# The MLPs of a two-layer decoder step, in two phases: the down product of 14 of 16 blocks by Strassen, with h through DRAM

## The reference, cut to what matters

```python
D_MODEL, D_FF = 1024, 4096

def sq_relu_mlp(x, w_up, w_down):
    h = jax.nn.relu(x @ w_up)
    return (h * h) @ w_down

for l in range(2):
    x = x + mixer(l, rmsnorm(x, norm_mix[l]))
    x = x + sq_relu_mlp(rmsnorm(x, norm_ffn[l]), w_up[l], w_down[l])
```

## Time and profile before

| | us |
|---|---|
| median of 3 runs | 2365.76 |
| lowest and highest run | 2365.53, 2367.63 |
| span of the profiled execution | 2366.2 |
| TensorE busy in it | 2313.8 |
| VectorE, ScalarE, GpSimd busy | 1476.8, 976.7, 317.2 |

### The profile page before, as it was taken

One profiled execution on the slowest core, in us unless ns is written; L12 is line 12 of the kernel. 1 busy time (PEld: TensorE's weight loads), 2 busy tenths in 40 slices (PEclk: granted clock), 3 DMA queues, 4 the chain that ended last, 5 costly groups with the idle time before them and its releaser, 6 DMA issues.

```text
span 2366.2 us, 41211 instructions
## 1 busy us (share of the span) xinstructions
PE 2313.8 (98%) x16214; PEld 2215.7 (94%) x16214; DVE 1476.8 (62%) x2598; ACT 976.7 (41%) x1978; POOL 317.2 (13%) x333
## 2 busy tenths in 40 slices
PE   7999999999999999999999999999999999999998
PEld 7988998878999999999999877869999999999998
DVE  6555555579766566565666666465856656556564
ACT  4232222235543353353434454254635335334345
POOL 1000000013111111111112011013011111111113
PEclk9999999999999999999999999999999999999999
DMA  4111121101111111211212311101111111121121
GB/s 128 37 50 57 50 69 40 46 29 45 46 54 36 53 53 35 62 44 36 66 50 56 98 28 53 36 10 45 36 54 54 36 58 48 35 63 44 44 62 74
DMA packets 160983, 119.71 MB, mean 51 GB/s; under 512 B 23623, under 2 KB 140276, under 8 KB 160836
## 3 DMA queue, kind: packets, MB, share of 16 engines
q1 hardware_dynamic: 160724, 118.10, 17.1%
q10 hardware_dynamic: 144, 0.02, 0.0%
HBM read 110.94 MB, written 12.33 MB: 52 GB/s over the span
## 4 chain that ended last, share of the span: by engine, by line
PE 72%; issue 20%; DVE 5%; POOL 1%; ACT 1%; DMA 0%; SPq 0%; POOLq 0%; DVEq 0%; ACTq 0%
PE acc L2634 9%; PE acc L2632 9%; PE acc L2633 9%; PE acc L2593 8%; PE acc L2592 8%; PE acc L2594 8%; PE acc L2701 3%; PE acc L2703 2%; PE acc L2702 2%; PE acc L2722 2%; PE acc L2570 1%; PE acc L2571 1%; PE acc L2572 1%; PE acc L2745 1%; PE acc L2733 1%
## 5 line engine op out<-in xcount | busy, mean ns | idle before, releaser
L2634 PE MATMUL acc<-h_hi,w_lo 128*128 128x352 f32 x1344 | 434.7, 323 | 0.0
L2632 PE MATMUL acc<-h_hi,w_hi 128*128 128x352 f32 x1344 | 434.0, 323 | 0.0
L2633 PE MATMUL acc<-h_lo,w_hi 128*128 128x352 f32 x1344 | 431.6, 321 | 0.0
L1535 DVE TENSOR_TENSOR x_res<-x_res,acc 128x1056 f32<-128x1056 f32 x224 | 280.6, 1253 | 126.2 <-PE acc L2634 126.0
L2633 PEld LDWEIGHTS acc<-h_lo,w_hi 128*128 128x128 f32 x1344 | 254.9, 190 | 0.0
L2593 PE MATMUL acc<-x_lo,w_hi 128*128 128x264 f32 x896 | 254.6, 284 | 0.0
L2594 PE MATMUL acc<-x_hi,w_lo 128*128 128x264 f32 x896 | 254.6, 284 | 0.0
L2592 PE MATMUL acc<-x_hi,w_hi 128*128 128x264 f32 x896 | 254.5, 284 | 0.0
L2632 PEld LDWEIGHTS acc<-h_hi,w_hi 128*128 128x128 f32 x1344 | 251.8, 187 | 0.0
L2634 PEld LDWEIGHTS acc<-h_hi,w_lo 128*128 128x128 f32 x1344 | 251.8, 187 | 0.0
L2349 PE MATMUL acc<-x_hi,w_hi 128*128 128x352 f32 x576 | 193.2, 335 | 1.4 <-DVE pair L1802 1.4
(11 more groups left out here) (351 smaller groups left out, 5356.7 us busy)
## 6 DMA issues: line engine op xcount, KB each, us to landing
w_raw<-in_w_up SPq DMA_DIRECT2D x64, 512.0 KB
w_raw<-in_w_down SPq DMA_DIRECT2D x64, 512.0 KB
w_raw<-in_w_mlstm_in SPq DMA_DIRECT2D x24, 512.0 KB
x_in<-in_x_prompt SPq DMA_DIRECT2D x8, 512.0 KB, 4.6
w_raw<-in_w_mlstm_out SPq DMA_DIRECT2D x8, 512.0 KB
w_raw<-in_w_q SPq DMA_DIRECT2D x16, 256.0 KB
w_raw<-in_w_attn_out SPq DMA_DIRECT2D x16, 256.0 KB
out_y_prompt<-y_out SPq DMA_DIRECT2D x8, 512.0 KB, 2.6
```

Of the source, the lines that this page charges most:

```text
L1535: V.tensor_tensor(blocks(x_res[:, k]), blocks(x_res[:, k]), row_banks(layer, k), ALU.add).then_inc(row_taken, 1)
L2632: T.matmul(out[:, b], hi[:, c], mh[:, span(b)], start=(c == 0), stop=False)
L2633: T.matmul(out[:, b], hi[:, c], ml[:, span(b)], start=False, stop=False)
L2634: x = T.matmul(out[:, b], lo[:, c], mh[:, span(b)], start=False, stop=(c == 1))
```

## The change

The MLP has two phases now, and its loops are written out. In the first, `up(f)` runs for all 16 blocks. The finished h (after relu, square and scale) goes to a DRAM tensor `h_rows` by two DMAs per block (`store_h`); `z_even` beside `act_a`/`act_b` gives each block's quarters a place of their own in turn.

In the second, the down product of blocks 0 to 13 is one Strassen product. The output's 1024 channels, the 14 blocks and the 1056 tokens are each cut in two. There are NPROD = 7 products, each over KG = 7 groups q of 256 rows; a group is 4 pairs of banks x 2 x 2 x 3 = 48 matmuls of 264 columns (`down(q)`). The table `DOWN` says for each product which quarter of the weights, with which other added or subtracted, meets which quarter of h, with which other, and into which quarters of `x_res` the result goes. Sums of weights are made by GpSimd (`down_sum`, 1024 columns), in products 0, 2, 4, 5 and 6; sums of h by VectorE (`t_sum_of_h`, 1056 columns), in products 1, 2, 3, 4 and 6. Both operands of each group are split by ScalarE (`w_high`, `t_high_of`) and VectorE (`w_low`, `t_low_of`). `w_hi`/`w_lo` hold two groups, the h operands have a ring of three.

SP loads three quarters of h into SBUF once (b11 in product 0, b12 in 2, b22 in 3) and streams the fourth (b21) in products 1 and 6. After each product VectorE adds every finished pair of banks, straight from PSUM, to one or two places of `x_res` (`add_banks`, 528 columns; 2, 2, 1, 2, 2, 2, 1 adds per pair for the seven products); ScalarE copies none of them out. The next product's first matmul into a pair waits for these adds (`bank_added`).

Blocks 14 and 15 stay plain and come last, as before in `last_rows` and `last_down`; their h is loaded back and split during products 5 and 6, their weights are steps 49 to 52 of the same step function.

The order of VectorE, ScalarE and SP in the down phase, and TensorE's waits:

```diff
+DOWN = (((1, 0), ADD, (1, 1), (0, 0), None, None, ((1, 0, ADD), (1, 1, SUB))),
...
+ADDS = [[(mh, nh, op, m) for m in range(4) for mh, nh, op in outs] for *_, outs in DOWN]
```

VectorE:

```diff
+            def down_step(layer, q):
+                w_low(layer, q)
+                if q + 1 < NG:
+                    t_low_of(layer, q + 1)
+                if q + 2 in T_SUMS:
+                    t_sum_of_h(layer, q + 2)
+                i, n = q // KG - 1, q % KG
+                if 0 <= i < NPROD - 1 and n < 2:
+                    outs = len(ADDS[i]) // 4
+                    for a in range(3 * n * outs, (3 + n) * outs):
+                        add_banks(layer, i, a)
+                if H_STEP < q <= H_STEP + 2 * TAIL:
+                    h_low(layer, q - H_STEP - 1)
...
+            def add_banks(layer, i, n):
+                mh, nh, op, m = ADDS[i][n]
+                if m < 3:
+                    dve.wait_ge(rows_done, 3 * (NPROD * layer + i) + m + 1)
+                else:
+                    dve.wait_ge(group_done, NG * layer + last_group(i) + 1)
+                rows = blocks(x_res[:, 4 * mh + m, HALVES[nh]], 2)
+                V.tensor_tensor(rows, rows, down_banks(layer, m), op).then_inc(bank_added, 1)
...
+                for q in range(2, NW):
+                    down_step(layer, q)
+                for n in range(len(ADDS[NPROD - 1])):
+                    add_banks(layer, NPROD - 1, n)
+                (last_rows, last_down)[layer]()
```

ScalarE:

```diff
+            def w_high(layer, q):
+                if q < 2:
+                    act.wait_ge(up_done, up_no(layer, NF - 1, 4 if q == 0 else 6))
+                else:
+                    act.wait_ge(group_done, NG * layer + min(q - 1, NG))
+                if q in W_SUMS:
+                    act.wait_ge(dw_sum, len(W_SUMS) * layer + W_SUMS.index(q) + 1)
...
+            def down_step(layer, q):
+                w_high(layer, q)
+                if q + 1 < NG:
+                    t_high_of(layer, q + 1)
+                if H_STEP <= q < H_STEP + 2 * TAIL:
+                    h_high(layer, q - H_STEP)
```

TensorE:

```diff
+                def down(q):
+                    i, g = divmod(q, KG)
+                    pe.wait_ge(dw_lo, NW * layer + q + 1)
+                    pe.wait_ge(dt_lo, NG * layer + q + 1)
+                    hi, lo = (w.rearrange("p (k m) -> p k m", k=2) for w in down_w(q))
+                    mh, ml = t_slot(q)
+                    for m in range(4):
+                        if g == 0 and i == 0:
+                            pe.wait_ge(z_dve, z_no(layer, NF - 1, ("C11", "C22", "C21", "C12")[m]))
+                        elif g == 0:
+                            pe.wait_ge(bank_added, bank_free(layer, i - 1, m))
```

SP:

```diff
+                def load_w(q):
...
+                    else:
+                        sp.wait_ge(dw_lo, NW * layer + q - 2)
...
+                load_h(0)
+                load_h(1)
+                load_h(2)
+                load_w(1)
+                load_h(3)
+                load_w(2)
+                store_h(NF - 1)
+                for q in range(3, NW):
+                    if q + 1 < NG:
+                        load_h(q + 1)
+                    load_w(q)
```

More of the change, by code:

```diff
@@ L230, in down_slot @@
[L230 to L255, removed]
+ENDS = [(k, (0,)) for k in range(4)] + [(k, (0, 1)) for k in range(4, 8)] + [(k, (1,)) for k in range(4)]
@@ L258, in build, with bank_free @@
+def bank_free(layer, product, m):
+    return ADDED[NPROD] * layer + ADDED[product] + (m + 1) * len(ADDS[product]) // 4
 def build(nc, io):
@@ L1363, in _ @@
+            def mlp(layer):
+                for f in range(PLAIN, NF):
+                    for j in (1, 3, 2, 6):
+                        weight_sum(layer, f, j)
+                for q in W_SUMS:
+                    down_sum(layer, q)
             nc.gpsimd.memset(eps_sum[:], DV * EPS).then_inc(ol_ready, 1)
@@ new lines, in mlp @@
+                plain_low(layer, 0, 1)
+                mean_first(1 + 2 * layer)
+                t_sums_of(layer, "T1")
+                mean_rest(1 + 2 * layer)
+                t_low(layer, "T1")
+                inverse(1 + 2 * layer)
+                plain_low(layer, 1, 0)
+                scaled(layer, 0, 1)
+                t_sums_of(layer, "T3")
+                scaled(layer, 0, 0)
+                plain_low(layer, 1, 1)
+                t_sums_of(layer, "T2")
+                t_low(layer, "T3")
@@ L2037, in up @@
+                t_sums_of(layer, "T4")
+                t_low(layer, "T2")
+                up_low(layer, 2, 0)
+                up_low(layer, 2, 1)
+                scaled(layer, 1, 1)
+                up_low(layer, 2, 2)
+                scaled(layer, 1, 0)
+                t_low(layer, "T4")
+                up_low(layer, 2, 3)
+                for f in range(PLAIN, NF):
+                    end = f == NF - 1
+                    up_low(layer, f, 4)
+                    up_low(layer, f, 5)
                     combine(layer, f, "U2")
+                    up_low(layer, f, 6)
@@ L2038, in up @@
                     combine(layer, f, "U3")
[L2039 to L2047 removed]
+                    if not end:
+                        up_low(layer, f + 1, 0)
+                    else:
+                        t_low_of(layer, 0)
@@ L2082, in mlp @@
-                walk_mlp(dve, layer, up, down, (last_rows, last_down)[layer])
+                        up_low(layer, f + 1, 3)
+                    scaled(layer, f, 1)
+                    if end:
+                        down_step(layer, 1)
+                    scaled(layer, f, 0)
+                for q in range(2, NW):
+                    down_step(layer, q)
+                for n in range(len(ADDS[NPROD - 1])):
+                    add_banks(layer, NPROD - 1, n)
+                (last_rows, last_down)[layer]()
@@ L2660, in last_rows @@
                         x.then_inc(row_done, 1)
-                walk_mlp(pe, layer, up, down, (last_rows, last_down)[layer])
+                for f in range(NF):
+                    up(f)
+                for q in range(NG):
+                    down(q)
+                (last_rows, last_down)[layer]()
             mlp(0)
```

823 lines of the change are left out of this document (418 added, 405 removed).

## The result

The changed kernel takes 2373.46 us (median of 10 runs, 2371.26 to 2378.85), the kernel before 2367.19 beside it (10 runs): ratio 1.0028, 95% interval 1.0019 to 1.0038. A second series gave 2375.32, ratio 1.0038 (1.0025 to 1.0052). The forecast was 2360, 6 us faster; the kernel became 6 us slower, clear of the interval. The time lies outside 2350 to 2370, where the prediction put its largest chance, inside its wide range of 2333 to 2390, and on the wrong side of the time before.

The account below looks back on a forecast made before the run. TensorE was taken as the bound, busy 2313.8 of 2366.2 us. Terms -78.8 + 43.4 + 12.8 + 5.8 - 1.5 + 12 = -6.3 gave 2360 us; range 2333 to 2390, with 0.42 for 2350 to 2370.

Parts of the forecast that it names:

- Columns, -78.8: Down products on TensorE: fewer columns, in matmuls of 264 instead of 352, save 39.4 us per layer, 78.8 in both.
- Up phase at nothing: Up blocks: VectorE, ScalarE and DMA work fits beside TensorE's 20.4 us per block, so the phase costs nothing.
- Between products, +43.4: Down-phase product boundaries: TensorE waits for VectorE's late x_res adds, 21.7 us per layer, 43.4 in all, bounds 31 to 53.
- End of the down phase, +12.8: Before the tails: last bank adds stand behind three weight splits, so TensorE waits 6.7 us in layer 0, 6.1 in layer 1.
- The stores of block 15, +5.8: From up to down: stores ahead in SP's queue delay the fourth group's weights, 2.9 us per layer, range 0 to 10.
- Second tail, -1.5: Layer 1's tail: TensorE's former 1.5 us idle for split weights goes, since all are ready.
- Granted clock, +12: After TensorE stalls the clock drops to 1.2 GHz: 12 stalls x 4/7 x 1.7 us, range 0 to 24.
- Rival 2: DMA becomes the bound in groups of products 0, 2 and 6: +31 us, 2391; chance 0.17.
- Rival 3: Every stall is dear: all collisions (53), all clock losses (24), stores at 10, giving 2386; chance 0.13.
- Rival 4: TensorE's unrolled program, 8141 to 14947 rows, loses time: 2373 if each layer loses 6 us; chance 0.05.
- Rival 1: Product boundaries: banks come free sooner, GpSimd never in VectorE's way: 2330, or 2338 with some clock loss; chance 0.18.
- rival 5: The bank adds between products do not bind, only the end stays: about 2305; chance 0.05.

Follow-up runs that it names:

- experiment 7: Changed kernel with only the fourth bank pair's adds moved ahead of the splits in VectorE's second step of a product: 2348.64 us, ratio 0.9914.
- Experiment 3: Changed kernel with only SP's two stores of h block 15 moved behind load_w(4): 2367.43 us, ratio 0.9999 to the kernel before.
- experiment 6: Changed kernel with GpSimd's weight sums cut to one column of 1024, so the output is wrong: 2350.74 us, ratio 0.9924.
- experiments 1: Changed kernel with all bank adds of a product in the next product's first step, t_sum behind the next split: 2340.78 us, ratio 0.9885.
- Experiment 8: Changed kernel with transposes nobody reads put into TensorE's waits: 2386.16 us; repeated on the kernel with only the fourth pair's adds moved: 2341.36 us.
- experiment 9: Kernel without waits: changed kernel with bank adds, tail adds and stores reordered, GpSimd's sums and VectorE's bank adds cut to one column: 2297.28 us.

## Why the forecast was wrong, point by point

- **Columns, -78.8.** Right in kind, 4.2 us too large. The step that failed here is the spacing of 0.1213, read from the up block and given to the down shape; the down shape takes 0.1222. Nothing in the profile before showed it, since the down shape ran there with 352 columns only.
- **Up phase at nothing.** Right: 333.3 us from the first up matmul to the first down matmul, in the changed kernel and in the one without waits alike.
- **Between products, +43.4.** The sum looks right: 37.9 us idle, 42.7 with 0.22 per wait. That is luck in part, for two errors cancel. The step that failed is the judgement by landings, in which GpSimd's sum collides surely at 3-4, by half at 1-2 and not at 5-6: the first-pair wait was 2.47 to 2.53 us at all three, in both layers, and 0.3 without GpSimd's sums. A boundary with both waits in full takes 5.0 us idle, 5.5 with 0.22 per wait (1081.50 and 1088.68), near the 5.8 forecast for it. But at the other five the clock fell behind the first wait, and the second came out at 1.0 to 1.6 us for 2.55, 6.7 us less in all. Without that the waits would have been some 49 us. The order of the second step held (experiment 7). Measured in the first layer were 2.9, 3.9, 1.1, 5.1, 3.2 and 4.2 idle, for 3.4, 4.6, 1.3, 5.8, 3.2 and 3.4. The upper bound of 26.5 per layer does not follow from the prediction's own costs: with all three collisions they make 25.3.
- **End of the down phase, +12.8.** Right: 6.6 and 6.0 us, forecast 6.7 and 6.1.
- **The stores of block 15, +5.8.** Too small: the waits for w_lo are 8.8 us, 9.7 with 0.22 per wait, inside the bound of 10. The weights of the fourth group were both landed 915.2 us into the run, 2.4 later than forecast, and 1.3 us at the second groups were not in the sum. Experiment 3 took the fourth group's wait away, experiment 6 did too: GpSimd's 2.4 us and SP's order each carry it.
- **Second tail, -1.5.** Right.
- **Granted clock, +12.** Too small: 20.7. The sum took 12 stalls at 4 in 7, and 26 waits of 2.4 us and more in two profiles gave 20. Nine stretches cost 15.0 us; the two at the ends last 6.8 us, of which 3.4 and 2.2 lie inside the wait, and cost 1.7 and 2.3. One more lies in the attention stage. The share of 4 in 7 came from pauses that were mostly shorter (1.5 to 2.2 us, one of 2.9) than the stalls it was used for, which are 2.5 and more, and one pause of 1.77 us at 452.53, with no fall behind it, was missing from the seven. The prediction also added each clock loss to the waits in full. Five of the stretches lie between the two waits of a boundary, and there the loss only took the place of waiting:

```profile
2165.52 0.36 PE L2753 MATMUL acc<-t_hi,w_hi 128*128 128x264 f32 x1 [2.53 <-DVE x_res L1694]
...
2172.71 0.39 PE L2753 MATMUL acc<-t_hi,w_hi 128*128 128x264 f32 x1 [1.05 <-DVE x_res L1694]
```

With a fall between them these two starts are 7.19 us apart; 1081.50 and 1088.68, without one, 7.18. At two of the five (992 and 1173) they are 7.4 and 7.8 us apart, because GpSimd's sum held the split behind the adds (1.46 and 1.83 us for 1.21). So the split between this term and the waits is one of booking. Together they were forecast at 55.4 and measured 63.4. Booked by cause, with the 6.7 us counted as waits, the waits are 6 us over their forecast and the clock 2.
- **Sum.** The misses are +4.2 columns, +3.9 stores, +8.7 clock, -0.7 boundaries, +0.2 ends and -1.6 at the start: +14.7. The forecast difference of -6.3 becomes +8.4; measured is +7.6. Every kind of loss was foreseen, apart from the trade between clock and wait; the sizes were not. The forecast stood 6 us from the time before on a sum of six terms, two of which were too small and one gain too large, so the sign rested on terms of 4 to 9 us.

**Rivals.** Rival 2, DMA as the bound, fell: the kernel without waits runs its down phases at 220 GB/s with no wait for w_lo, and the window at 1088.80 shows 397 GB/s over 3.2 us. Rival 3, every stall dear, had the direction and most of the terms right: stores at 10, clock near its upper end, and all collisions. It came out at 2386 mainly because it, too, added the clock losses to the full waits, and because its bound of 53 was too large. Rival 4, unrolled code, fell with the kernel without waits. Rival 1, in which GpSimd never stands in the way, fell with the first-pair waits and experiment 6; rival 5, adds that do not bind, with the 37.9 us of waits and experiments 1 and 7.

## What to carry to other kernels

When work is moved behind a few late signals, write out the other engine's queue for the steps around each signal: some 43 of the 75 us that the narrower products gained went to adds that stood behind splits nobody needed yet, GpSimd's hold on these splits included, and reordering them, with two other moves and one in the DMA queue, turned 0.3% slower into 2.5% faster. Count TensorE's stalls of 2.4 us and more and charge most of them with 1.7 us of clock (20 of 26 in the two profiles of the changed kernel), unless another wait close behind takes the loss up, as at five boundaries here (1.0 to 1.6 us of wait for 2.55). A sum of large terms that nearly cancel gives no sign: a forecast of -6 built on -79 and +73 is "about the same", and its chances should say so.

## What the runs showed of the chip that I had not expected

- A stretch at clock 0.50 between two waits for the same engine cost next to nothing: it only made TensorE arrive later at the second wait. At boundaries of the changed kernel where the clock fell for 3.4 us behind the first wait, the second is 1.0 to 1.6 us; where it did not, 2.55. In experiment 8 work put into the first wait made the kernel slower, 2386.16 for 2373.46.
- Matmuls of 264 columns with the same three-fold pattern take 0.1222 us start to start in the down products and 0.1213 in the up products, at clock 1.00 and with no idle time. Why was not found. It does not hang on VectorE's or GpSimd's load: in the changed kernel, with VectorE busy 25 and GpSimd 6 of 30 us from 1010, and in experiment 9, with VectorE at 171 of 287 and GpSimd at 15 to 17, it is 0.1222. DMA is not excluded: its share is 0.61 to 0.63 in these stretches and 0.33 in the up phase.
- GpSimd's sum is held up by VectorE too: 2.88 us instead of 2.39 when called 0.6 us before the end of a VectorE split (985.57, experiment 6).
